# A hybrid encoder step on one core: adaLN group 5 multiplied behind the first expert loop

## The reference, cut to what matters

```python
def _adaln(c, w, b, n):
    return jnp.split(jax.nn.silu(c) @ w + b, n, axis=-1)
...
for layer in range(DEPTH):
    sh1, sc1, g1, sh2, sc2, g2 = _adaln(c, ada_w[layer], ada_b[layer], 6)
    if layer < N_A_LAYERS:
        ...  # trailing-mean mixer
    else:
        if shared is None:
            shared = _shared_kv(x, c, past, kv_ada_w, kv_ada_b, kv_norm, w_kvf, b_f, k_norm)
        h = _modulate(x, norm_g[layer, 0], sh1, sc1)
        y = _fox_mixer(h, shared, start_pos, w_q[j], q_norm[j], w_o[j])
    x = x + g1[:, None, :] * y
    h = _modulate(x, norm_g[layer, 1], sh2, sc2)
    x = x + g2[:, None, :] * _moe(h, w_router, b_router, w_gate[layer], w_up[layer], w_down[layer])
```

## Time and profile before

| | |
|---|---|
| median of 3 runs | 1396.0 us (1395.11 to 1398.91) |
| profiled execution | 1394.58 us, its span 1393.0 us |
| busy share of the span | PE 81%, DVE 30%, ACT 17%, POOL 14% |
| mean granted TensorE clock | 0.91 of full speed |
| DMA | 360.67 MB, 259 GB/s over the span |

### The profile page before, as it was taken

One profiled execution on the slowest core, in us unless ns is written; L12 is line 12 of the kernel. 1 busy time (PEld: TensorE's weight loads), 2 busy tenths in 40 slices (PEclk: granted clock), 3 DMA queues, 4 the chain that ended last, 5 costly groups with the idle time before them and its releaser, 6 DMA issues.

```text
span 1393.0 us, 12312 instructions
## 1 busy us (share of the span) xinstructions
PE 1125.0 (81%) x4632; PEld 541.5 (39%) x4632; DVE 411.6 (30%) x880; ACT 238.2 (17%) x499; POOL 189.0 (14%) x322
## 2 busy tenths in 40 slices
PE   3898189999999919999977985589708999999990
PEld 0455044444443414445543542344404444344340
DVE  3545700000000064362165652123560101000005
ACT  2121010000000022221125651111201001000001
POOL 6100210000000030000118631010030000000002
PEclk8987689999999959999997998799858999999995
DMA  9999778999998941132423019865335899998925
GB/s 365 379 421 377 302 224 339 422 361 373 426 336 346 378 144 54 61 103 84 172 77 108 1 34 357 291 204 234 140 130 195 348 424 346 383 420 315 373 105 207
DMA packets 57210, 360.67 MB, mean 259 GB/s; under 512 B 7300, under 2 KB 7796, under 8 KB 39149
## 3 DMA queue, kind: packets, MB, share of 16 engines
q1 hardware_dynamic: 35712, 285.79, 52.1%
q0 software_dynamic: 19904, 73.58, 15.3%
q10 hardware_dynamic: 1532, 0.49, 0.1%
HBM read 330.26 MB, written 34.29 MB: 262 GB/s over the span
## 4 chain that ended last, share of the span: by engine, by line
PE 72%; DMA 9%; DVE 9%; POOL 4%; issue 3%; ACT 2%; SPq 1%; ACTq 0%; POOLq 0%; DVEq 0%
PE pb L889 31%; PE pb L1071 16%; PE pb L891 9%; DMA ring<-in_ada_w_dram 4%; DMA h<-in_ada_w_dram 3%; PE pb L800 2%; POOL ring L764 2%; PE pb L883 2%; PE pb L830 2%; PE pb L1020 1%; DVE h L1845 1%; POOL xs_d L668 1%; PE pb L1163 1%; PE pb L918 1%; PE pb L1075 1%
## 5 line engine op out<-in xcount | busy, mean ns | idle before, releaser
L889 PE MATMUL pb<-ring,h 128*128 128x512 f32 x640 | 290.9, 604 | 19.7 <-DVE h L1845 19.7
L1071 PE MATMUL pb<-ring,hT_raw 128*128 128x512 f32 x512 | 224.7, 596 | 1.3 <-DVE hT_raw L1658 0.8
L889 PEld LDWEIGHTS pb<-ring,h 128*128 128x128 f32 x640 | 120.1, 193 | 163.2 <-issue 163.2
L889 PE MATMUL pb<-ring,hT_raw 128*128 128x512 f32 x320 | 143.1, 600 | 1.5 <-issue 1.5
L1071 PEld LDWEIGHTS pb<-ring,hT_raw 128*128 128x128 f32 x512 | 96.6, 191 | 116.3 <-issue 114.7
L1859 DVE COPY hT_raw<-pb 128x512 f32<-128x512 f32 x26 | 18.0, 692 | 378.7 <-PE pb L889 288.9
L889 PEld LDWEIGHTS pb<-ring,hT_raw 128*128 128x128 f32 x320 | 60.7, 192 | 80.5 <-issue 80.5
L700 POOL DMA_DIRECT2D ys_d<-hT_raw x26 | 14.1, 541 | 574.0 <-DVE hT_raw L1859 574.0
L891 PE MATMUL pb<-ring,h 128*64 128x512 f32 x384 | 86.4, 596 | 5.9 <-DVE h L1845 5.9
L800 PE MATMUL pb<-ring,cT 128*32 128x512 f32 x384 | 53.6, 689 | 29.3 <-DMA ring<-in_ada_w_dram 29.3
L1853 DVE TENSOR_TENSOR h<-pb,h 128x512 f32<-128x512 f32 x26 | 18.0, 692 | 183.6 <-PE pb L889 145.6
(11 more groups left out here) (333 smaller groups left out, 1152.9 us busy)
## 6 DMA issues: line engine op xcount, KB each, us to landing
ring<-in_w_up_dram SPq DMA_DIRECT2D x32, 2048.0 KB, 11.3
ring<-in_w_down_dram SPq DMA_DIRECT2D x32, 2048.0 KB, 11.6
ring<-in_w_gate_dram SPq DMA_DIRECT2D x32, 2048.0 KB, 9.7
ring<-in_ada_w_dram SPq DMA_DIRECT2D x16, 2048.0 KB, 10.6
ys_d<-hT_raw POOLq DMA_DIRECT2D x26, 512.0 KB, 10.3
h<-xs_d POOLq DMA_DIRECT2D x20, 512.0 KB, 13.8
ring<-in_kv_ada_w_dram SPq DMA_DIRECT2D x4, 2048.0 KB, 9.9
ring<-in_w_kvf_dram SPq DMA_DIRECT2D x4, 2048.0 KB, 16.0
```

What stands on the lines that cost most here:

```text
L889: return T.matmul(bank[:, :], lhs, rhs[0], start=start, stop=stop)
L1071: last = T.matmul(bank[:, :], hT[:, k, col[t]:col[t] + P], w[:, k * 512:(k + 1) * 512], start=(k == 0), stop=(k == KC - 1))
```

## The change

Group 5 joins the ring: its four units are loaded into slots 0, 2, 1 and 4 as the last steps of the first expert loop leave them, and are multiplied on PE right behind that loop, into bank 7. SP's issues stand inside its refill list (units 20 and 21 after the up refills of step 10, the other two behind the list). DVE adds the bias before tile 1 of the combine, ACT stores before tile 2. The gathered rows go to other slots (3, 5 and 4), the last tile's after group 5 is multiplied. The projection's first two loads wait for the units in their slots and for the gather of tiles 0 and 1. In the sample attention only group 6 is left, at three first places and one second place; SP issues its first two units, then both loads of `w_o`, then the last two units.

```diff
...
-    EARLY = 20
-    ada_slot = [n % 6 for n in range(EARLY)]
-    before0 = [ada_slot.count(s) for s in range(6)]
-    unit_count = [n // 6 + 1 for n in range(EARLY)] + [(n - EARLY) // 2 + 1 for n in range(EARLY, NADA)]
-    before_proj = [n + NPE for n in before0]
+    EARLY, LATE = 20, 24
+    ada_slot = [n % 6 for n in range(EARLY)] + [0, 2, 1, 4]
+    before0 = [ada_slot[:EARLY].count(s) for s in range(6)]
+    unit_count = [ada_slot[:n + 1].count(ada_slot[n]) + (NPE if n >= EARLY else 0) for n in range(LATE)] \
+        + [(n - LATE) // 2 + 1 for n in range(LATE, NADA)]
+    before_proj = [ada_slot.count(s) + NPE for s in range(6)]
...
-        yg = rf[:, 8192:8192 + NT * 2 * D].rearrange("p (t r n) -> p t r n", t=NT, r=2)
+        yg = [rf[:, c:c + 2 * D].rearrange("p (r n) -> p r n", r=2) for c in (12288, 14336, 20480, 22528, 16384)]
...
-                a = (n - EARLY) % 2
-                if n - EARLY >= 2:
+                a = (n - LATE) % 2
+                if n - LATE >= 2:
...
                     for q in STEP_PLACES[n]:
                         if q + 2 < NE:
                             refill(kind, q + 2)
+                    if layer == 0 and kind == "u" and n == PLACE_STEP[NE - 3]:
+                        sp.wait_ge(E.gate, PLACE_STEP[NE - 2] + 1)
+                        load(ada_slot[EARLY], ada_src[EARLY])
+                        sp.wait_ge(E.up, PLACE_STEP[NE - 2] + 1)
+                        load(ada_slot[EARLY + 1], ada_src[EARLY + 1])
+                if layer == 0:
+                    sp.wait_ge(E.gate, PLACE_STEP[NE - 1] + 1)
+                    load(ada_slot[EARLY + 2], ada_src[EARLY + 2])
+                    sp.wait_ge(E.down, 2 * PLACE_STEP[NE - 2] + 2)
+                    load(ada_slot[EARLY + 3], ada_src[EARLY + 3])
                 with sp.If(n_ov > 0):
+                    if layer == 0:
+                        sp.wait_ge(unit_used, LATE)
...
             experts(0)
             for n in range(6):
                 if n < 2:
-                    sp.wait_ge(E.gate, PLACE_STEP[NE - 2 + n] + 1)
+                    sp.wait_ge(unit_used, EARLY + 2 * n + 1)
+                    sp.wait_ge(yg_loaded[n], 32)
...
-            for n in range(EARLY, EARLY + 3):
+            for n in range(LATE, LATE + 2):
-            for n in range(EARLY + 3, NADA):
+            for n in range(LATE + 2, NADA):
...
                 for t in range(NT):
+                    if layer == 0 and t == TS:
+                        pool.wait_ge(unit_used, LATE)
-                            out=yg[0:rows[t], t, r, :], out_offset=None, in_=ys_d[:, :],
+                            out=yg[t][0:rows[t], r, :], out_offset=None, in_=ys_d[:, :],
...
-                bank = pb[grp % 2] if grp < 5 else pb[6]
+                bank = pb[grp % 2] if grp < 5 else pb[12 - grp]
-                    if n < EARLY:
+                    if n < LATE:
...
                     pe_down(g, units(D_SLOT, n))
+                if layer == 0:
+                    ada(5)
...
-                ada(5 + gi // 2, [2 * (gi % 2)])
+                if gi:
+                    ada(6, [gi - 1])
                 pe.wait_ge(sa_exp, gi + 1)
...
-                ada(5 + gi // 2, [2 * (gi % 2) + 1])
+                if gi == 3:
+                    ada(6, [3])
                 pe.wait_ge(sa_loaded[par], 80 * (gi // 2 + 1))
...
-                                (stage[s:P:32, grp % 2, :] if grp < 5 else gmul[s:P:32, grp % 2, :])).then_inc(ada_stored[grp], 16)
+                                (stage[s:P:32, grp % 2, :] if grp < 6 else gmul[s:P:32, grp % 2, :])).then_inc(ada_stored[grp], 16)
...
+                    if layer == 0 and t == 2:
+                        store_ada(5)
-                    A.activation(yg[0:rows[t], t, 0, :], yg[0:rows[t], t, 0, :], ACT.Copy,
+                    A.activation(yg[t][0:rows[t], 0, :], yg[t][0:rows[t], 0, :], ACT.Copy,
...
-                if gi == 1:
-                    store_ada(5)
...
             def stage_ada(grp):
-                if grp == 4:
-                    dve.wait_ge(ada_stored[2], 32)
+                if grp in (4, 5):
+                    dve.wait_ge(ada_stored[grp - 2], 32)
...
-                bank = pb[grp % 2] if grp < 5 else pb[6]
-                row = stage if grp < 5 else gmul
+                bank = pb[grp % 2] if grp < 5 else pb[12 - grp]
+                row = stage if grp < 6 else gmul
...
+                    if layer == 0 and t == 1:
+                        stage_ada(5)
-                    y0, y1 = yg[0:r, t, 0, :], yg[0:r, t, 1, :]
+                    y0, y1 = yg[t][0:r, 0, :], yg[t][0:r, 1, :]
...
-                if gi == 1:
-                    stage_ada(5)
```

## The result

The changed kernel takes 1387.48 us (median of 5 runs, 1381.53 to 1388.81), beside 1395.89 us (1394.23 to 1398.91) for the kernel before: a ratio of 0.9929 [0.9914, 0.9944]. It is faster, as forecast, but by 8.4 us and not by 22; the time lies above the predicted range of 1364 to 1385. The profiled execution took 1387.48 us with a span of 1385.9, which is 7.1 less than the span of before.

The account below looks back on a forecast made before the run. TensorE was taken to carry most of the chain, so time is saved only where it waits. The terms -31.8 + 2 + 8.9 + 0.7 = -20.2 us took 1394.6 to 1374.4; predicted 1374, range 1364 to 1385.

Parts of the forecast that it names:

- Part 2: Unit loads in the first expert loop: w_down late, stall 7.5 us plus 1.4 us slow start, costing 8.9 us.
- the prediction's own sign of being wrong: Wrong if the roughly 7 us gap before down of step 11 is absent or doubled, or waits appear elsewhere.
- The row of 16.3 us: Profile row for a load issued directly behind another of its size; taken as w_down's landing time, giving 7.5 us stall.
- the one of 22.8 us: Profile row of the second w_down, behind one load and beside the row fill; upper bound, stall 14.0 us.
- Part 1: Sample attention: units 20 to 23 leave, gaining 31.8 us; less 2 us waiting for unit 27, 29.8 us.
- the sign of being right: Among other signs, gi 0's scores to the output projection should span near 67 us instead of 98.
- the second rival: Wait moves inside the sample attention: unit 27 or a key load behind w_o is late; 1382.6 us, chance 0.12.
- Part 3: Group 5's product behind the expert loop: 7.7 us hidden in 23.98 us idle; only 0.7 us lost to VectorE's bias add.
- Part 4: Projection's first load, held until about 510.9 us, has 20.9 us and needs 18.7: nothing lost, at most 10.2 us.
- the in-time load: Rival at the expert loop's tail: the w_down load lands in time, no 8.9 us cost; 1365.5 us, chance 0.15.
- the late projection load: Rival: the projection's first load takes 31.1 us against 20.9 allowed; 1384.6 us, chance 0.08.
- no gain: Rival: w_o's bytes set the sample attention's end, so the time stays at 1394.6 us; chance 0.03.

Follow-up runs that it names:

- the split of w_o: Changed kernel with the second half of w_o loaded behind units 26 and 27 in SyncE's list: 1383.92 us, ratio 0.9923.
- SyncE's order mended: Changed kernel with unit 21's load and its wait moved behind the two w_down refills in SyncE's list: 1371.17 us, ratio 0.9835.
- 1386.17: Changed kernel with only the row fill of ys_d moved from step 11 of the expert loop to step 1: 1386.17 us in one execution.
- 1378.76: Changed kernel with unit 21's load moved behind the w_down refills, its wait still ahead of them: 1378.76 us in one execution.
- 1376.21: Changed kernel with unit 21's load behind the w_down refills, its wait still ahead, and the row fill at step 1: 1376.21 us in one execution.
- filler: Unused identity products in softmax gaps: 1369.9 us added to unit 21 behind the refills; halved, added to that plus split w_o, 1364.49 us.

## Why the prediction was right in its direction and wrong in its size

The forecast was -20.2 us against the profiled execution; measured is -7.1. The difference of 13.1 us lies in these places.

- **Part 2, the wait and its place: right. Its size: the step that failed.** The gap stands before down of step 11, released by the w_down load behind unit 21's wait, as written. The failing step is "I take 16.3 us, since the new place is that of a second load and the fill has a five-microsecond start this time. The stall is 7.5 us". The load took 21.7 us, the gap was 12.9 us, and the slow start behind it 2.6 us in place of 1.4: 15.6 us where 8.9 were counted, 6.7 us off. By the prediction's own sign of being wrong, a gap doubled, it came near: about 7 us were named. The fill's start did not help. In the changed kernel from 450 to 469 us GpSimd's queue, which carries the fill, moved 4.72 MB and took 71% of the DMA engines' time, SyncE's queue 1.88 MB and 27.5%. Windows just before and just after the fill had landed (at 468.9 us):

```profile
456.00:462.00 6.00, 5.01 (x20) 2.83 (x19) 1.32 (x2) 0.70 (x2) 0.00 (x0) 1.00 0.92 298
462.00:468.00 6.00, 3.29 (x8) 1.14 (x6) 0.00 (x0) 0.49 (x1) 0.00 (x0) 1.00 0.88 300
469.00:475.00 6.00, 0.00 (x0) 0.00 (x0) 0.00 (x0) 0.00 (x0) 0.00 (x0) 0.55 1.03 441
```

  The DMA engines are about as busy in all three windows, but by the trace they move 298 and 300 GB/s beside the fill and 441 after it. That rate is not fixed by the fill: before the change, with the same fill in flight, windows from 452 to 469 us have 375, 519 and 430 GB/s. The row of 16.3 us that the step was taken from has no fill beside it, and the one of 22.8 us that has one was used as a far bound only. By resemblance it was the nearer row: the new place has both the load ahead and the fill.

- **Part 1, the waits that go: right. Two small terms: wrong.** The sample attention is 25.2 us shorter in place of 29.8 (73.4 us from gi 0's scores to the output projection, where the sign of being right said 67 and the prediction's own sum makes 68.8). Unit 27 costs 4.8 us in place of 2: in the timeline above, 4.00 us of wait in place of VectorE's 0.97, then 3.34 us for 1.92, and some 0.3 us in the products around it. The cause of the wait is the second rival's, w_o ahead of the last units, which the split of w_o shows; the slow rate is not w_o's, since with the split and no such wait unit 27 still takes 3.58 us. And the clock, taken as 0 "because the softmax gaps stay", has a cost: the transposes take 1.6, 0.2 and 1.7 us longer (3.4 in all), while the values' products and small pieces give about 1.6 back (3.62 us for the 4.60 of gi 1, for one). The net is 1.8 us. Together 2.8 + 1.8 = 4.6 us, the whole difference. The softmax gaps did stay, but in gi 0 the unit that ended the gap did not; it had taken the slow rate on itself, 3.64 us, and the transposes behind it then ran fast. In gi 2 that does not serve: a unit of 1.92 us and a wait of 1.65 stand ahead of the transposes in both kernels, and they take 1.97 us before and 3.63 after. What decides there was not found; the gap just ahead alone does not.

- **Behind the sample attention** nothing was predicted, and 2.1 us were lost, 1.7 of them in the output projection (43.13 us for 41.44), the clock again: 0.62 in its first 4 us, 1.00 before the change.

- **Part 3: right.** The product costs nothing. From down of step 12 to the first projection 0.6 us were lost, 0.7 predicted.

- **Part 4: right.** The projection's first load went out at 516.7 us, landed after 16.0 and was not waited for.

So 6.7 + 4.6 + 2.1 = 13.4 us were lost against the forecast; with the rest, +0.7 between the projections and the scores, -1.0 ahead of the tail and -0.1 in the combine, this is the 13.1 up to rounding. Of the rivals, the in-time load, the late projection load and "no gain" did not come; the wait that moves came in part, on top of a larger stall. The range was made from one miss at a time, and here two came with the same sign. With SyncE's order mended 1371.17 was measured. That this is close to the forecast's 1374 is luck: the 1374 holds 8.9 us of a stall that this version does not have, and without it the same sum gives 1365.5.

Still open: what, besides the gap just ahead, sets the clock of the transposes in gi 2; whether the versions with one execution (1386.17, 1378.76 and 1376.21) keep their distances to a microsecond or two; and what a filler costs that is just long enough.

## What to carry to other kernels

When a load with a wait of its own is put into an in-order queue, place it behind every refill whose condition comes true earlier; here that one move was worth 16.3 us, twice the gain of the change as it stood. To price a load at a new place, choose the row that shares everything with it, the copies on other queues too, not only its place in its own queue. And where work is taken out of short waits, look at what runs next: here the three groups of transposes took 3.4 us longer at the lower clock, and a prediction that puts this at nothing needs a reason from the trace.

## What was not expected of the hardware

- A DRAM-to-DRAM copy of 4.2 MB on GpSimd's queue delayed a 2.1 MB load on SyncE's queue, issued 5 us and more behind it, by 9.1 to 9.7 us, against 4.0 to 4.6 for a whole load of 2.1 MB directly ahead of it in the same queue. A load issued 1.9 us ahead of the copy landed after 8.9 and 11.2 us, where 8.0 is the time without copy and load ahead.
- The 16 key transposes take 1.97 or about 3.6 us, at a granted clock of 1.00 or of 0.51 to 0.52, and work put into the gap before them changes which. In gi 0 of the changed kernel nothing ran for 3.51 us (3.55 us at 0.52); with 3.39 us of unused products there they take 1.97. In gi 1 and gi 2 one unit of 1.92 us and a wait of 1.65 left them slow, and the unit and 1.60 us of filler kept them fast. The gap just before does not decide alone: in gi 2 of the kernel before the same unit and the same wait left them at 1.97 us.
